# A hybrid decoder step on one core: memory scores inside the attention's tail, the first roots ahead of the page numbers, and the first piece of each sample step ahead of the recurrence's finish

## The chip, the cores and the metric

The program runs on one core of one Trainium2 chip. Its time is device microseconds for one execution of the whole step, from the first to the last instruction with the little that lies around it. The engines are TensorE (PE, with its weight loads as PEld), VectorE (DVE), ScalarE (ACT), GpSimd (POOL) and the queue engine SyncE (SP). A measurement is the median of three runs.

## What is computed

Two layers, each on 2048 prompt rows and on 8 sample rows (one new token for each of eight sequences). A layer normalises its input, projects it to 3360 columns, and feeds four head groups: a short gated convolution, an RWKV-7 recurrence, latent attention (causal for the prompt, over 4096 cached tokens for the samples), and cross-attention into 256 memory tokens. Cut to what matters here:

```
for l in range(DEPTH):
    mk, mv = mem_kv(mem_prompt, mem_norm_g[l], w_mem_k[l], w_mem_v[l])      # rms_norm, two projections
    xp, ... = trunk_layer(xp, pos_p, ..., mk, mv, prompt_attend, p)
    ckv_past = cache_ckv[l, page_table].reshape(Bs, -1, KV_RANK)
    xs, ... = trunk_layer(xs, pos_s, ..., cache_mem_k[l], cache_mem_v[l], make_sample_attend(...), p)

def mem_attend(q, mem_k, mem_v):
    s = jnp.einsum('bshd,bmhd->bhsm', qh, mem_k).astype(jnp.float32) * (HEAD_DIM ** -0.5)
    pr = jax.nn.softmax(s, axis=-1).astype(q.dtype)
    return jnp.einsum('bhsm,bmhd->bshd', pr, mem_v).reshape(B, S, MEM_W)

mixed = concat([conv_out * silu(c_gate), rwkv_out * silu(r_gate), mla_out * silu(mla_gate), mem_out * silu(mem_gate)])
x = x + rms_norm(einsum('bse,ed->bsd', mixed, w_out), post_g)
```

## The kernel before

Each engine has its own program, written out by hand; engines meet only through semaphores (`s_...`). The order of an engine's work is the order of its code. A layer is a prologue and eight blocks of 256 prompt rows (`block(B, m, e)`, with `m = 0..3`, `e = 0, 1`, block number `2m + e`), then a short pass for the samples. "Block 4 of layer 0" below is `m = 2, e = 0`.

**A block on PE** is `project`, `rwkv_chunks`, `attention`, `attention_out`, `memory`, `project_out`. PE is a line of small fp32 matmuls. In the traces all of them stand at line 815 (`mm`) or, for transposes, at line 819 (`tr`), so they are told apart by their tiles: `bank<-kv,Q` are attention scores, `bank<-cst,Sm` the transposes of probabilities (`turn(c)`), `bank<-memKT,mq` the memory's scores, `bank<-kv,cst` and `bank<-kv,wuq` the products of a sample step. Some instructions have two records each.

**The attention** of a block works through `n = 8(m+1)` chunks of scores. `scores(c)` fills one of five banks in rotation (`score_bank`: 0, 1, 7, 6, 5); DVE takes the row maximum (`masked_max`), ACT the exponentials (`probs`, L2645, into `Sm`), PE turns them (`turn(c)`, which waits for `probs(c)`), ACT copies them out (`take(c)`, L2655 to L2667) and PE multiplies with the values (`values(x)`). PE runs five chunks of scores ahead. In the last five chunks there are no scores left to issue between two turns: this is the tail. ACT alternates `probs(c+1)` and `take(c)`. In the blocks with `m = 0`, `take(4)` also waits for `values(0)`.

**Behind the tail**, `attention_out` (L1217) issues `memory_scores(B, 0)` and `(B, 1)` into banks 0, 1 and 6, 7, the recurrence's mean (`group_norm`), two gate tiles (25 and 26) and, between them, four transposes of `T3` into bank 5, which wait for `s_on`: DVE has to have the inverse row sums ready. DVE's `memory_max(B, j)` comes after its attention work and the inverse sums (L2277). `memory` turns the memory's probabilities and multiplies with `memV`. `project_out` multiplies eight row groups `k` with `w_out`, in the order of `i0 = 0..7`; the weights for `i0 = 4` are loaded once `i0 = 0` is done.

**Sample steps.** The samples' work is spread over the blocks: PE does it between two groups of `project_out` (`sample_step`), DVE after `rwkv_finish`. Block 0: squares (L2000, L2001), PE sums them at `i0 = 1`, POOL takes the roots (L2862), DVE scales, PE projects the queries at `i0 = 3`. Block 1: keys (L2041 to L2054), summed at `i0 = 2`. Blocks 2 and 3: `spread` (L2103), used at `i0 = 2`. `rwkv_finish` (L1894 to L1901) starts when ACT has the inverse root of the variance (L2552), and its result is needed at `i0 = 6`.

**Prologue of layer 0.** DVE scales the mean squares of the memory rows (L1569), POOL raises them to the power -1/2 (`memory_roots`, L2776), DVE scales the rows (L1571), PE turns them (`turn_memory`), DVE copies them out with their gain (L1580), and PE makes the memory's keys and values with `w_mem_k` and `w_mem_v`. On POOL, four loads of the page numbers and their conversion (L2765, L2767) stand ahead of those roots; the conversion waits for the loads. The numbers are first used by POOL's own `gather` in block 0's recurrence.

Of the kernel before, what the change touches and what calls it, by code (L numbers as in the profile page):

```python
# [19 lines left out]
P = 128  # L20
# [141 lines left out]
def build_program(nc, a):  # L162
    ctx = ExitStack()
    with ctx:
# [383 lines left out]
        def score_bank(c):  # L548

            return (0, 1, 7, 6, 5)[c % 5]  # L550

# [261 lines left out]
        def _(pe):  # L813
# [347 lines left out]
            def attention(B, l, m, e):  # L1161
# [55 lines left out]
            def attention_out(B):  # L1217

                if B.prompt:
                    memory_scores(B, 0)  # L1220
                    memory_scores(B, 1)
# [3 lines left out]
                    for i in range(4):  # L1225
                        last = tr(PP[5][:, i * P:(i + 1) * P], flat3(T3)[:, i * P:(i + 1) * P], P)
# [9 lines left out]
            def memory_scores(B, j):  # L1236
                J = slice(j * P, (j + 1) * P)
                for h in range(2):
                    q = slice(64 * h, 64 * h + 64)
                    for p in range(2):  # L1240
                        last = mm(PP[6 * j + h][:, p * NM:(p + 1) * NM], mq[q, p, J], memKT[q, p, :])
                last.then_inc(s_ms.h, 1)

            def memory(B):
                def turn(j):
                    pe.wait_ge(s_mn.h, s_mn.at(B.ip, j + 1))
                    b0 = 6 * j
                    for q in range(4):
                        for t in range(2):
                            last = tr(PP[b0 + q // 2][:, (q % 2) * T + t * P:(q % 2) * T + (t + 1) * P],  # L1250
# [294 lines left out]
        def _(v):  # L1545
# [357 lines left out]
            def attention(B, l, m, e):  # L1903
# [37 lines left out]
            def gate_attention(B):  # L1941
                n = B.n
                v.wait_ge(s_uv.h, s_uv.at(B.ot, 1))
                if B.prompt:
# [3 lines left out]
                    v.tensor_tensor(x, x, halves(5, n), MULT).then_inc(s_uvr.h, 1)  # L1948
# [4 lines left out]
            def memory_max(B, j):  # L1953
                top, neg, _, _ = mst[j]
                v.wait_ge(s_ms.h, s_ms.at(B.ip, j + 1))
                for h in range(2):
                    v.tensor_reduce(top[:, 2 * h:2 * h + 2], halves(6 * j + h, T), AX, MAX)
# [37 lines left out]

            def sample_latents(B, scaled):

                l, n = B.l, NS
                v.wait_ge(s_pa.h, s_pa.at(B.ip, NTILES))
                v.tensor_tensor(ssq[:, 0, :], sproj[:, 7, :], sproj[:, 7, :], MULT)  # L2000
                v.tensor_tensor(ssq[:, 1:3, :], sproj[:, 9:11, :], sproj[:, 9:11, :], MULT).then_inc(s_sdv.h, 1)  # L2001
# [35 lines left out]
            def sample_prepare(B, scaled):  # L2037

                l = B.l
# [9 lines left out]
                kx, rx = spr[:, 2:4, :], spr[:, 0:2, :]  # L2049
                drain()  # L2050
                v.tensor_tensor(sT1, kx, scalars(V("kk", 0, 2), NS), MULT)
                v.tensor_tensor(su, sproj[:, 15:17, :], sproj[:, 13:15, :], MULT)
                drain()
                v.tensor_tensor(sT2, sT1, sT1, MULT).then_inc(s_sdv.h, 1)  # L2054
# [52 lines left out]
            def sample_states(B, steps, turned):  # L2107

                l = B.l
                if steps[0] == 0:  # L2110
                    v.wait_ge(s_sac.h, s_sac.at(l, SAC["decay"]))
                    v.wait_ge(s_sl.h, s_sl.at(l, s_sl.n))
                for i in steps:
                    spread(l, i)
# [131 lines left out]
            for l in range(L):  # L2246
# [26 lines left out]
                def block(B, m, e):  # L2273
# [3 lines left out]
                    memory_max(B, 0)  # L2277
# [623 lines left out]
```

## Time and profile before

| | us |
|---|---|
| runs of before | 3522.21, 3518.31, 3515.10 (median 3518.31) |
| the profiled execution | 3512.8 |
| its span, first to last instruction | 3511.0 |
| PE busy in it | 3400.2 (97%) |
| DVE / ACT / POOL busy | 2023.6 / 1267.0 / 243.9 |

The profiled execution is 5.5 us faster than the median of the three runs. A row of the timeline gives start, duration, engine, line, operation, output and inputs; the bracket at its end is the time that the engine was idle before it, and what released it.

### The profile page before, as it was taken

The numbers are of one execution on the slowest core, as the hardware profiler recorded it, in microseconds if no ns is written. First come the engines' busy times: TensorE is split into PE (matmuls) and PEld (weight loads), VectorE is DVE, ScalarE is ACT, GpSimd is POOL, SyncE is SP. The second block draws the span as 40 slices with busy tenths as digits, with TensorE's granted clock in tenths as the row PEclk, the third lists the DMA queues.
The fourth block names the chain that finished last, engine by engine and source line by source line (L and its number), as shares of the span: only waits on it lengthen the run. The fifth ranks groups of instructions, "written<-read, shape, count | busy, mean of one in ns | idle before, by whom it ended". The sixth has DMA issues, their size and how long they took to land.

```text
span 3511.0 us, 80468 instructions
## 1 busy us (share of the span) xinstructions
PE 3400.2 (97%) x33076; PEld 2591.2 (74%) x33076; DVE 2023.6 (58%) x5212; ACT 1267.0 (36%) x3599; POOL 243.9 (7%) x284
## 2 busy tenths in 40 slices
PE   7999999999999999999999999999999999999998
PEld 5768686877869678686567786868778687776864
DVE  3656565665656556565356566656656565464653
ACT  2323334242343423524433233332423434234343
POOL 3200100000010000000040001000000000000000
PEclk9999999999999999999999999999999999999999
DMA  7654453625436153252365634536263351632512
GB/s 218 208 175 158 144 189 108 200 88 184 135 122 206 51 200 123 102 192 69 106 216 174 201 127 173 155 115 210 63 231 115 117 186 49 236 110 91 194 55 68
DMA packets 281024, 514.82 MB, mean 147 GB/s; under 512 B 30037, under 2 KB 215571, under 8 KB 268115
## 3 DMA queue, kind: packets, MB, share of 16 engines
q1 hardware_dynamic: 258903, 463.96, 40.3%
q0 software_dynamic: 11648, 41.95, 3.4%
q8 instruction: 263, 4.31, 0.5%
q10 hardware_dynamic: 10108, 3.76, 0.4%
q14 instruction: 102, 0.84, 0.1%
HBM read 473.15 MB, written 47.49 MB: 148 GB/s over the span
## 4 chain that ended last, share of the span: by engine, by line
PE 86%; ACT 5%; DVE 4%; issue 2%; DMA 2%; DVEq 1%; ACTq 1%; POOL 0%; SPq 0%; POOLq 0%
PE bank L815 78%; PE bank L819 7%; DVEq L1548 1%; DMA win<-in_w_in 1%; DMA wout<-in_w_out 1%; ACT Q L2575 1%; ACT PT L2690 0%; ACT Sm L2645 0%; ACT qr L2574 0%; DVE mix L1778 0%; ACTq L2551 0%; ACT L2552 0%; ACT Q L2573 0%; DVE swaa L1776 0%; DVE mix L1774 0%
## 5 line engine op out<-in xcount | busy, mean ns | idle before, releaser
L815 PE MATMUL bank<-hT,win 128*128 128x256 f32 (+3 forms) x6384 | 1188.1, 339 | 5.4 <-DMA win<-in_w_in 2.7
L815 PEld LDWEIGHTS bank<-hT,win 128*128 128x128 f32 (+1 forms) x6384 | 949.2, 186 | 143.1 <-issue 34.7
L815 PE MATMUL bank<-wout,win 128*128 128x128 f32 x3136 | 379.9, 276 | 0.0
L815 PEld LDWEIGHTS bank<-wout,win 128*128 128x128 f32 x3136 | 364.6, 192 | 1.0
L815 PE MATMUL bank<-kv,Q 96*128 96x512 f32 (+3 forms) x640 | 276.4, 529 | 0.2
L1915 DVE TENSOR_REDUCE ml<-bank 128x1 f32<-128x512 f32 (+3 forms) x320 | 195.3, 610 | 124.1 <-PE bank L815 113.7
L819 PEld LDWEIGHTS bank<-cst,Sm 128*128 128x128 f32 x1344 | 157.6, 141 | 145.9 <-issue 67.4
L819 PE MATMUL bank<-cst,Sm 128*128 128x128 f32 x1344 | 210.7, 278 | 24.9 <-ACT Sm L2645 18.0
L2645 ACT ACTIVATE Sm<-bank,ml 128x512 f32<-128x512 f32 (+3 forms) x320 | 200.1, 626 | 76.8 <-DVE ml L1920 70.8
L815 PE MATMUL bank<-wout,mix 128*128 128x512 f32 x480 | 218.4, 605 | 2.2 <-DMA wout<-in_w_out 1.3
L815 PEld LDWEIGHTS bank<-wout,mix 128*128 128x128 f32 x480 | 89.8, 192 | 109.6 <-issue 107.9
L2541 ACT ACTIVATE mix<-bank 128x512 f32<-128x512 f32 (+1 forms) x68 | 39.7, 597 | 351.3 <-PE bank L815 351.3
L2421 ACT ACTIVATE mix<-bank 128x256 f32<-128x256 f32 x128 | 49.2, 384 | 307.8 <-PE bank L815 307.8
L2820 POOL DMA_INDIRECT G<-in_cache_ckv,idc x32 | 31.7, 989 | 1574.6 <-PE bank L815 1569.7
L815 PEld LDWEIGHTS bank<-kv,Q 96*128 96x128 f32 x640 | 101.4, 192 | 22.8 <-issue 15.0
L2428 ACT ACTIVATE mix<-bank 128x128 f32<-128x128 f32 x98 | 27.0, 276 | 227.8 <-PE bank L815 209.9
L815 PE MATMUL bank<-PT,XX 64*64 64x64 f32 x2560 | 100.7, 231 | 7.4 <-ACT PT L2584 4.3
L815 PE MATMUL bank<-PT,mix 128*128 128x512 f32 x224 | 102.7, 602 | 0.0
L815 PE MATMUL bank<-XX,mix 128*128 128x512 f32 x224 | 101.3, 595 | 0.0
L815 PE MATMUL bank<-XX,PT 64*64 64x64 f32 x2048 | 93.1, 218 | 0.0
L815 PEld LDWEIGHTS bank<-PT,XX 64*64 64x64 f32 x2560 | 71.0, 133 | 27.4 <-ACT PT L2584 21.4
L1802 DVE TENSOR_TENSOR OO<-OO,cst 128x256 f32<-128x256 f32 x160 | 63.6, 422 | 47.0 <-PE bank L815 43.4
(527 smaller groups left out, 5952.3 us busy)
## 6 DMA issues: line engine op xcount, KB each, us to landing
win<-wfast SPq DMA_DIRECT2D x98, 1024.0 KB, 6.7
win<-in_w_in SPq DMA_DIRECT2D x78, 1024.0 KB, 5.6
win<-wfast SPq DMA_DIRECT2D x98, 768.0 KB, 6.1
wout<-in_w_out SPq DMA_DIRECT2D x60, 512.0 KB, 7.8
out_xres<-xin SPq DMA_DIRECT2D x16, 1024.0 KB
win<-in_w_in SPq DMA_DIRECT2D x16, 896.0 KB, 4.9
PT<-in_w_out SPq DMA_DIRECT2D x28, 512.0 KB, 3.8
XX<-in_w_out SPq DMA_DIRECT2D x28, 512.0 KB, 4.6
```

The source lines that it names most:

```text
L815: return pe.matmul(out, lhsT, rhs, start=start, stop=stop, skip_group_check=True)
L819: return pe.transpose(out, in_, ident[0:w, 0:w])
L1548: v.drain()
L1802: v.tensor_tensor(Om[j], An[j], mlev[:, lev + 1:lev + 2, :].broadcast_to([P, NH, 64]), MULT).then_inc(s_om.h, 1)
L1915: v.tensor_reduce(top, bank[:, 0:w], AX, MAX)
L2421: act.activation(o, PP[bank][0:o.shape[0], 0:T], ACT.Copy).then_inc(s_pa.h, tiles)
L2428: act.activation(first[i % 2], PP[tile_bank(PAIRS[i])][:, 0:P], ACT.Copy).then_inc(s_p1.h, 1)
L2541: last = act.activation(junk[0:w, (2 * j + i) * 512:(2 * j + i + 1) * 512], PP[B.bank + 2 * j + i][r0 * i:r0 * i + w, :], ACT.Square, accu ...
L2575: act.activation(Q96[NOPE:NOPE + RD, H, :], x[NOPE + RD:P], ACT.Copy).then_inc(s_qpr.h, 1)
L2645: act.activation(Sm[:, c % 2, 0:w], PP[score_bank(c)][:, 0:w], ACT.Exp, bias=rneg[:, row:row + 1], scale=MLA_SCALE, accum_out=psum[:, row, ...
L2820: pool.indirect_dma_start(dst, None, a[cache].rearrange("l n (g k) r -> (l n g) (k r)", g=g), bass.IndirectOffsetOnAxis(ap=idc[:, q, b:b + ...
```

## The change

Three edits, all in the order of work; nothing is computed otherwise.

1. `memory_scores(B, 0)` follows `turn(n - 4)` and `memory_scores(B, 1)` follows `turn(n - 2)`, in the banks that the chunks `n - 5` to `n - 2` have left; the transposes of `T3` go to the bank of chunk `n - 1`. DVE's two `memory_max` move ahead of the inverse sums.
2. POOL takes the roots of memory and of the first rows before it converts the page numbers.
3. `sample_head` does the first piece of a sample step (squares; keys; `spread(0)` or `spread(3)`) ahead of `memory_out` and `rwkv_finish`.

```diff
+        def freed_banks(m):
+            return [score_bank(8 * (m + 1) + i) for i in range(5)]
+        def memory_bank(m, j, h):
+            return freed_banks(m)[2 * j + h]
...
                     if c + 5 < n:
                         scores(c + 5)
+                    if c in (n - 4, n - 2):
+                        memory_scores(B, (c - n + 4) // 2)
                     if c > m and (c - m) % 4 == 0:
...
                 if B.prompt:
-                    memory_scores(B, 0)
-                    memory_scores(B, 1)
                     group_norm(B, 0)
                     tile(B, 25)
                     pe.wait_ge(s_on.h, s_on.at(B.ip, 1))
                     for i in range(4):
-                        last = tr(PP[5][:, i * P:(i + 1) * P], flat3(T3)[:, i * P:(i + 1) * P], P)
+                        last = tr(PP[freed_banks(B.m)[4]][:, i * P:(i + 1) * P], flat3(T3)[:, i * P:(i + 1) * P], P)
...
                         scale_rows(B, scaled)
                         scaled += 1
+                memory_max(B, 0)
+                memory_max(B, 1)
                 v.wait_ge(s_ae.h, n0 + n)
                 v.tensor_reduce(rsum, psum[:, :, 0:m + 1], AX, ADD)
...
+            def sample_head(B):
+                l = B.l
+                if B.block == 0:
+                    latent_squares(B)
+                elif B.block == 1:
+                    sample_keys(l)
+                elif B.block in (2, 3):
+                    if B.block == 2:
+                        v.wait_ge(s_sac.h, s_sac.at(l, SAC["decay"]))
+                    spread(l, 0 if B.block == 2 else 3)
...
                     if B.block > 3 and B.turns:
                         turn_rows(B, 0, 8)
+                    sample_head(B)
                     memory_out(B)
                     rwkv_finish(B)
...
-            pool.wait_ge(s_pg.h, 16 * 4)
-            pool.tensor_copy(pgf[:, :], pgi[:, :])
-            pool.drain()
-            pool.tensor_scalar(pgf[:, :], pgf[:, :], 4.0, K("sub"), MULT, ADD)
-            pool.drain()
...
                 x_roots(l * IT, 1)
                 x_roots(l * IT + 1)
 
+                if l == 0:
+                    pool.wait_ge(s_pg.h, 16 * 4)
+                    pool.tensor_copy(pgf[:, :], pgi[:, :])
+                    pool.drain()
+                    pool.tensor_scalar(pgf[:, :], pgf[:, :], 4.0, K("sub"), MULT, ADD)
+                    pool.drain()
```

`latent_squares` is the wait for the projections and the two squares of `sample_latents`; `sample_keys` is the head of `sample_prepare` up to the squares of the keys, without the convolution's product. Both go out of their old places.

On PE, the tail of block 4 of layer 0 (24 chunks). `Sm` are turned probabilities of chunks 19 to 23, four, four, two, four and four transposes; `memKT,mq` are the memory's scores. Before:

```order
2239 L819 MATMUL bank3<-cst,Sm 128x128 x4
2240 L819 MATMUL bank2<-cst,Sm 128x128 x4
2241 L819 MATMUL bank3<-cst,Sm 128x128 x2
2242 L819 MATMUL bank2<-cst,Sm 128x128 x4
...
2255 L819 MATMUL bank3<-cst,Sm 128x128 x4
...
2272 L815 MATMUL bank0<-memKT,mq 128x256 x2
2273 L815 MATMUL bank1<-memKT,mq 128x256 x2
2274 L815 MATMUL bank6<-memKT,mq 128x256 x2
2275 L815 MATMUL bank7<-memKT,mq 128x256 x2
2276 L815 MATMUL bank2<-cxs,cst 128x512
```

The same place in the changed kernel:

```order
2239 L827 MATMUL bank3<-cst,Sm 128x128 x4
2240 L827 MATMUL bank2<-cst,Sm 128x128 x4
2241 L823 MATMUL bank5<-memKT,mq 128x256 x2
2242 L823 MATMUL bank0<-memKT,mq 128x256 x2
2243 L827 MATMUL bank3<-cst,Sm 128x128 x2
2244 L827 MATMUL bank2<-cst,Sm 128x128 x4
2245 L823 MATMUL bank1<-memKT,mq 128x256 x2
2246 L823 MATMUL bank7<-memKT,mq 128x256 x2
...
2276 L823 MATMUL bank2<-cxs,cst 128x512
```

Half of the memory's scores now stands between the turns of chunks 20 and 21, half behind that of chunk 22; the mean's product (`cxs,cst`) follows the last values at once.

On DVE, the end of block 1 of layer 0, from the gate of the memory group (`mix<-Bp,mix`) to the keys of the samples (`raw`, `kv`). Before:

```order
503 L1784 SCALAR_TENSOR_TENSOR mix<-Bp,mix 128x512 [waits gate_tanh_ready]
504 L1970 SCALAR_TENSOR_TENSOR mix<-mix,bank 128x512 [waits mem_values_done]
505 L1894 TENSOR_TENSOR cxs<-cxs,T 128x512 [waits square_root_done]
...
508 L1901 SCALAR_TENSOR_TENSOR mix<-mix,cxs 128x512
509 L2041 COPY raw<-sproj 128x16 x3
510 L2042 COPY raw<-sproj 128x8
511 L2044 TENSOR_TENSOR kv<-shs,raw 128x56
```

After:

```order
503 L1791 SCALAR_TENSOR_TENSOR mix<-Bp,mix 128x512 [waits gate_tanh_ready]
504 L2064 COPY raw<-sproj 128x16 x3
505 L2065 COPY raw<-sproj 128x8
506 L2067 TENSOR_TENSOR kv<-shs,raw 128x56
...
510 L2076 TENSOR_TENSOR kv<-kv 128x16
511 L1979 SCALAR_TENSOR_TENSOR mix<-mix,bank 128x512 [waits mem_values_done]
512 L1901 TENSOR_TENSOR cxs<-cxs,T 128x512 [waits square_root_done]
```

The keys and their squares stand ahead of the instruction that waits for `square_root_done`, where they stood behind it.

## Rows read from the trace of the kernel before

**Rows 1.** The page: busy time of each engine.

```profile
PE 3400.2 (97%) x33076; PEld 2591.2 (74%) x33076; DVE 2023.6 (58%) x5212; ACT 1267.0 (36%) x3599; POOL 243.9 (7%) x284
```

**Rows 2.** Waits of PE, whole span: us in total, times, longest.

```profile
PE bank L819 <- ACT Sm L2645: 18.0, 32, 1.1
...
PE bank L815 <- DVE kv L2001: 6.5, 2, 3.2
PE bank L815 <- DVE kv L2103: 3.9, 4, 1.0
...
PE bank L815 <- ACT XX L2655: 1.1, 4, 0.3
```

**Rows 3.** Timelines of DVE, POOL and PE in the prologue.

```profile
11.21 0.15 DVE L1569 TENSOR_SCALAR st<-st 128x1 f32<-128x1 f32 x1
...
15.34 0.19 POOL L2765 CAST pgf<-pgi 128x8 f32<-128x8 int32 x1 [6.41 <-DMA pgi<-in_page_table]
...
16.57 0.58 POOL L2776 TENSOR_TENSOR st<-st,mhalf 128x1 f32<-128x1 f32 x1 [0.15 <-issue]
...
17.98 3.68 PE L819 MATMUL bank<-cst,hT 128*128 128x128 f32 x16 [7.54 <-DVE hT L1571]
22.54 12.55 PE L815 MATMUL bank<-kv 128*128 128x512 f32 x24 [0.88 <-DVE kv L1580]
```

**Rows 4.** Issue and landing (us from issue) of the memory's value weights.

```profile
3.38 1.63 SPq L583 DMA_DIRECT2D kv<-in_w_mem_v  x1
...
kv<-in_w_mem_v SPq DMA_DIRECT2D x1, 1024.0 KB, 13.4
```

**Rows 5.** Timelines of PE and DVE: tail of block 4, then a turn outside tails.

```profile
1004.66 0.44 PE L819 MATMUL bank<-cst,Sm 128*128 128x128 f32 x2 [0.71 <-ACT Sm L2645]
1005.82 0.66 PE L819 MATMUL bank<-cst,Sm 128*128 128x128 f32 x4 [0.72 <-ACT Sm L2645]
...
1007.62 0.43 DVE L1938 COPY T<-ml 128x512 f32<-128x512 f32 x1 [0.42 <-PE bank L815]
...
1010.35 2.10 PE L815 MATMUL bank<-memKT,mq 64*128 64x256 f32 x16
...
1016.80 0.60 PE L819 MATMUL bank<-cst,T 128*128 128x128 f32 x4
...
1414.30 0.33 PE L819 MATMUL bank<-cst,Sm 128*128 128x128 f32 x1 [0.64 <-ACT Sm L2645]
```

**Rows 6.** Timeline of ACT, block 1: `take(4)`.

```profile
378.66 0.38 ACT L2664 ACTIVATE T<-bank 128x256 f32<-128x256 f32 x1 [0.21 <-PE bank L815]
```

**Rows 7.** Timeline of PE in `project_out` of blocks 0 and 1, layer 1 last.

```profile
206.68 0.81 PE L815 MATMUL bank<-kv,cst 128*128 128x8 f32 x6 [3.24 <-DVE kv L2001]
207.34 5.38 PE L815 MATMUL bank<-wout,mix 128*128 128x512 f32 x8
212.55 3.60 PE L815 MATMUL bank<-PT,mix 128*128 128x512 f32 x8
215.99 1.85 PE L815 MATMUL bank<-kv,wuq 128*128 128x8 f32 x16
...
407.59 0.37 PE L815 MATMUL bank<-kv,cst 128*128 128x16 f32 x2 [1.43 <-DVE kv L2054]
...
2148.31 0.37 PE L815 MATMUL bank<-kv,cst 128*128 128x16 f32 x2 [1.73 <-DVE kv L2054]
```

**Rows 8.** Stretches: busy time of PE, PEld, DVE, ACT, POOL; then granted clock.

```profile
208.00:210.00 2.00, 2.00 (x4) 0.75 (x3) 0.00 (x0) 0.00 (x0) 2.00 (x1) 0.50 0.99 411
...
410.00:412.00 2.00, 2.00 (x6) 0.95 (x5) 1.92 (x6) 0.00 (x0) 2.00 (x1) 1.00 1.06 420
...
2150.00:2152.00 2.00, 2.00 (x4) 0.85 (x3) 2.00 (x7) 0.00 (x0) 1.90 (x1) 0.50 1.01 404
```

**Rows 9.** Timelines of DVE and POOL, block 0: recurrence's finish, roots.

```profile
203.33 0.69 DVE L1894 TENSOR_TENSOR cxs<-cxs,T 128x512 f32<-128x512 f32 x1 [2.46 <-ACT T L2552]
...
207.85 2.93 POOL L2862 TENSOR_TENSOR kv<-kv,mhalf 128x16 f32<-128x16 f32 x1 [5.42 <-DVE kv L2010]
```

More of the change, by code:

```diff
@@ L1240, in memory_scores @@
                     for p in range(2):
-                        last = mm(PP[6 * j + h][:, p * NM:(p + 1) * NM], mq[q, p, J], memKT[q, p, :])
+                        last = mm(PP[memory_bank(B.m, j, h)][:, p * NM:(p + 1) * NM], mq[q, p, J], memKT[q, p, :])
                 last.then_inc(s_ms.h, 1)
@@ L1246, in turn @@
                     pe.wait_ge(s_mn.h, s_mn.at(B.ip, j + 1))
-                    b0 = 6 * j
                     for q in range(4):
                         for t in range(2):
-                            last = tr(PP[b0 + q // 2][:, (q % 2) * T + t * P:(q % 2) * T + (t + 1) * P],
+                            last = tr(PP[memory_bank(B.m, j, q // 2)][:, (q % 2) * T + t * P:(q % 2) * T + (t + 1) * P],
                                       Pm[j][:, q, t * P:(t + 1) * P], P)
@@ L1947, in gate_attention @@
                     drain()
-                    v.tensor_tensor(x, x, halves(5, n), MULT).then_inc(s_uvr.h, 1)
+                    v.tensor_tensor(x, x, halves(freed_banks(B.m)[4], n), MULT).then_inc(s_uvr.h, 1)
                     return
@@ L1956, in memory_max @@
                 for h in range(2):
[L1957 removed]
+                    v.tensor_reduce(top[:, 2 * h:2 * h + 2], halves(memory_bank(B.m, j, h), T), AX, MAX)
                 drain()
@@ L1994, in residual, with latent_squares @@
                     drain()
-            def sample_latents(B, scaled):
-                l, n = B.l, NS
+            def sample_head(B):
[8 more added lines that the diff above has]
+                    spread(l, 0 if B.block == 2 else 3)
+            def latent_squares(B):
                 v.wait_ge(s_pa.h, s_pa.at(B.ip, NTILES))
@@ L2001, in sample_latents @@
                 v.tensor_tensor(ssq[:, 1:3, :], sproj[:, 9:11, :], sproj[:, 9:11, :], MULT).then_inc(s_sdv.h, 1)
+            def sample_latents(B, scaled):
+                l, n = B.l, NS
                 v.tensor_copy(smq[:, :, :], sproj[:, 11:13, :])
@@ L2035, in sample_latents, with sample_keys @@
                 drain()
-            def sample_prepare(B, scaled):
-                l = B.l
+            def sample_keys(l):
                 for i, t in ((0, 3), (2, 1), (4, 5)):
@@ L2048, in sample_prepare @@
                 v.tensor_tensor(spr, raw[:, :, :], sT3, ADD).then_inc(s_sdv.h, 1)
-                kx, rx = spr[:, 2:4, :], spr[:, 0:2, :]
+                kx = spr[:, 2:4, :]
                 drain()
                 v.tensor_tensor(sT1, kx, scalars(V("kk", 0, 2), NS), MULT)
+                drain()
+                v.tensor_tensor(sT2, sT1, sT1, MULT).then_inc(s_sdv.h, 1)
+            def sample_prepare(B, scaled):
+                l = B.l
+                kx, rx = spr[:, 2:4, :], spr[:, 0:2, :]
                 v.tensor_tensor(su, sproj[:, 15:17, :], sproj[:, 13:15, :], MULT)
                 drain()
-                v.tensor_tensor(sT2, sT1, sT1, MULT).then_inc(s_sdv.h, 1)
                 for p in range(2):
@@ L2110, in sample_states @@
                 if steps[0] == 0:
-                    v.wait_ge(s_sac.h, s_sac.at(l, SAC["decay"]))
                     v.wait_ge(s_sl.h, s_sl.at(l, s_sl.n))
                 for i in steps:
-                    spread(l, i)
+                    if i != steps[0]:
+                        spread(l, i)
                     if i in turned:
@@ L2276, in block @@
                     scaled = attention(B, l, m, e)
-                    memory_max(B, 0)
-                    memory_max(B, 1)
                     centre(B)
@@ L2682, in block @@
                         for q in range(4):
-                            last = act.activation(Pm[j][:, q, :], PP[6 * j + q // 2][:, (q % 2) * T:(q % 2) * T + T], ACT.Exp,
+                            last = act.activation(Pm[j][:, q, :], PP[memory_bank(m, j, q // 2)][:, (q % 2) * T:(q % 2) * T + T], ACT.Exp,
                                                   bias=mst[j][1][:, q:q + 1], scale=MEM_SCALE, accum_out=mst[j][2][:, q:q + 1])
@@ L2689, in block @@
                         for q in range(2):
-                            last = act.activation(PTm[j][:, q, :, :], PP[6 * j + q][:, :].rearrange("p (a t) -> p a t", a=4), ACT.Copy)
+                            last = act.activation(PTm[j][:, q, :, :], PP[memory_bank(m, j, q)][:, :].rearrange("p (a t) -> p a t", a=4), ACT.Copy)
                         last.then_inc(s_mtr.h, 1)
```

## The prediction

> **What bounds the kernel now.** I read the busy times first: PE works 3400.2 of 3511.0 us, every other engine under 60% [rows 1]. So only two things can shorten the run: PE's idle time, 111 us in all, and PE's own slow stretches. Next I read the list of PE's waits, of which the edits aim at the largest [rows 2], then the timelines around each, to see what the waiting engine's releaser was itself waiting for, and last the granted clock in the stretches where the same product takes two different times [rows 7, 8]. The diff keeps every product, so PE's 3400.2 us stay but for the clock.
>
> **Edit 2, the roots in the prologue.** DVE's mean squares are there at 11.21 + 0.15 = 11.36, but POOL begins the root at 16.57 [rows 3]. In between stands the conversion of the page numbers, which waited 6.41 us for its transfer and began at 15.34. With the root ahead it can begin at about 11.45: 5.1 us earlier. Everything behind is a chain (DVE's scaling, PE's turns after 7.54 us idle, DVE's copies, the keys' and values' products at 22.54), and the compute rows down that chain give no other wait, so the 5.1 go through. Two things could cut it. The products would begin at 22.54 − 5.1 = 17.4, and the value weights land at 3.38 + 13.4 = 16.8 [rows 4]: 0.6 to spare. The conversion now follows the last root and delays POOL's later sums of the first block by about a microsecond; what they feed leaves through the queue, and PE asks for it in the recurrence, microseconds later: nothing. The page numbers are used in block 0's recurrence. If transfers bind instead I bound the gain below by 2, a landing 3.7 later with products not before 20.5, and above by 5.2, the whole distance from 11.36 to 16.57. I take **−5.1**.
>
> **Edit 1, memory's scores in the tail.** PE waits 18.0 us for probabilities, 32 times [rows 2]. Going through the turns block by block, 28 of them lie in tails; the four others are 0.64 [rows 5] and 0.42, in both layers, 2.1 us, which leaves 15.8 in tails. In the tail ACT needs about as long for `probs(c+1)` and `take(c)` as PE for a turn and its values, or longer, and PE has nothing to put between. The memory's scores last 2.10 us, 1.05 for each half [rows 5]. They are work that PE has to do anyway, so a wait of up to 1.05 in front of which a half stands vanishes. In blocks 0 to 3, 6 and 7 a half covers what it stands ahead of. In block 4 the waits are 0.71 and 0.72 [rows 5], in block 5 together as much, and in each of them both lie between the turns n−4 and n−2, where only the first half stands: 1.43 − 1.05 = 0.38 is left, four times, −1.5. In blocks 0 and 1 `take(4)` already waits 0.21 for the values [rows 6], and those now come behind a half: I charge 0.3 in the two tails where it is latest, in each layer one, −0.6. The four waits for `take`'s last copies, 1.1 [rows 2], end in the same stretch and are covered by the second half. Sum 15.8 − 1.5 − 0.6 + 1.1 = **−14.8**. Upper bound 15.8 + 1.1 = 17. Lower bound 7: each half could shift the wait to the next turn, because what binds is ACT's chain and not PE's order; then only the waits at the second half's place and behind it go, about half.
>
> The edit moves DVE's two `memory_max` ahead of the inverse sums, on which the transposes of `T3` wait. In block 4 DVE starts the copy for them at 1007.62 and PE turns them at 1016.80 [rows 5]. The second maximum now needs the second half, over at about 1008, and some 1.5 us of DVE; sums, inverse and copy take another 1.5: ready at some 1011. PE does the same work ahead of these transposes in another order, without the waits of 1.43 us, and comes there at 1016.80 − 1.43 = 1015.4. Some 4 us are left: cost nothing. The banks are those of chunks whose probabilities have been taken before the turn ahead.
>
> **Edit 3, the first pieces of the sample steps.** The waits that it aims at are 6.5 (squares, twice 3.24), 3.2 (keys, 1.43 and 1.73) and 3.9 (`spread`, four of about 0.98) [rows 2, 7]: 13.6. In each DVE did the piece behind `rwkv_finish`, which lasts from 203.33 to about 206.3 in block 0, and which itself waited 2.46 us for ACT [rows 9]. In that idle time fit the squares (about 0.3), `spread` (about 1.4) and nearly the keys (about 1.9): so neither `memory_out`'s product, which PE needs only at `i0 = 4`, nor `rwkv_finish`, needed at `i0 = 6`, comes later. All 13.6 go.
>
> The clock is the second gain. After the wait of 3.24 the eight products that follow take 5.38 and the next eight 3.60 [rows 7], and the granted clock of that stretch is 0.50, the 1.2 GHz level, where it is 1.00 (2.4 GHz) after the wait of 1.43 [rows 8]. It is 0.50 again after the wait of 1.73 in block 1 of layer 1 [rows 8]. With block 0 of layer 1 that is three falls, each worth 5.38 − 3.60 = 1.78: 5.3 us, which go when the waits do.
> The Trainium skill ("TensorE: Matmul & The Clock Gate", section "Why this matters for your kernels") advises to leave no idle gap of PE above about 3 µs, since one such drops the clock. By it the two gaps of 3.24 explain a fall and that of 1.73 does not, so a third fall would stay: the sum would be 1.8 less, about 3482. The trace shows the fall behind 1.73 as well, and I go by the trace.
>
> Against it a new wait. The queries at `i0 = 3` need the roots, 9.31 us behind the squares' sums (215.99 − 206.68) [rows 7], 7.5 with the clock up. The sums now come at 203.44, so PE is at the queries at about 210.95. DVE takes the sums up only behind `rwkv_finish`, as before at 207.6, POOL's root takes 2.93 from 207.85 [rows 9], and DVE's scaling ends at about 211.2. New wait 0.3, twice: −0.6. The weights of `i0 = 4`, ordered when `i0 = 0` is done, have until then 14.3 us, as now in blocks without a wait, where they cost 0.7 at most; that goes in the range. Sum 13.6 + 5.3 − 0.6 = **−18.3**, bounds 13.0 (no clock back) and 18.9.
>
> **Sum.** 5.1 + 14.8 + 18.3 = 38.2. The profiled execution took 3512.8, so 3474.6; the median of the runs stands 5.5 above it, so **3480** for the median. With all lower bounds, 22, it is 3496, with all upper ones, 5.2 + 17 + 18.9 = 41.1, it is 3477. The three runs of before lie 7 us apart; I allow 3 for a median.
>
> **Rivals.**
> The tail gives half. Each half of the scores delays the values behind it, so ACT's `take` and with it the next `probs` come later, and the wait stands again one turn further on. For it: `take(4)` is already waiting [rows 6], and in block 4 two waits follow each other [rows 5]. Against: ACT has in the tail only `probs` and `take`, and `take(c)` needs the turn alone, not the values, except in the blocks with `m = 0`. 7.4 lost: 3487, chance 0.12.
> The prologue is bound by transfers. The value weights leave 0.6 [rows 4], and a landing later by 2 to 3 us than before gives 3483; chance 0.07.
> The clock is not gained, because other short waits of the same stretch (the new one at the queries) make it fall: 5.3 lost, 3485; chance 0.08.
> Slower: the inverse sums come too late. They stand behind both maxima, and the second maximum behind PE's second half. Once they slip by more than the 4 us of margin, PE waits for them in all 16 blocks; the gain of 38.2 is gone at 38.2 / 16 = 2.4 us a block, a slip of 4 + 2.4 = 6.4 in place of the 3 that I work out. At a slip of 7.6 it is 3.6 a block, 57.6 − 38.2 = 19 slower: 3537. For it: the copy for these transposes starts at 1007.62 only after 0.42 us of waiting for PE [rows 5], so DVE has no lead there. Against: from 1011 to 1015.4 two more maxima would fit. Chance 0.03.
> The order doesn't bind as I read it, and everything that goes from the waits comes back elsewhere in the same block (PT's or the gates' copies on ACT, transfers of weights): within 0.2%; chance 0.02.
>
> **How the numbers follow.** My forecast has 0.68, the three rivals that are faster than before too 0.12 + 0.07 + 0.08 = 0.27, the two last 0.05. 0.2% is 7 us, about what a measurement of this kernel can tell from no change; the forecast lies 38 below, and even all lower bounds leave 22. So faster has 0.95, within 0.02, slower 0.03. The likeliest case gives 3480 with 3474 to 3486 by its unknown costs and the spread of the medians; the range reaches to the rivals at 3483 to 3487 and to a pair of them together at 3492: 3471 to 3493; outside it I leave the two last cases and, of the others, sizes beyond their bounds.
>
> **What would show it.** In the changed profile PE's list should have no wait for the squares or keys and at most a few tenths for `spread`; its wait for probabilities should fall from 18.0 to about 4, of which 2.1 outside the tails and 1.5 in blocks 4 and 5. PE's first transposes should stand at about 12.9 instead of 17.98. In the stretches of `project_out` of blocks 0 and 1 the clock should read 1.00 and eight products 3.60. A new row of about 0.3, for the scaled squares, should stand in block 0. `T3`'s transposes should have no wait. I am wrong if the probabilities' wait stays above 9, if a wait for the inverse sums appears in many blocks, or if PE's busy time doesn't fall by about 5 us.

## The result and the profile after

| | before | after |
|---|---|---|
| median of four runs each, us | 3516.70 | 3479.70 |
| lowest and highest, us | 3513.84, 3522.21 | 3477.17, 3481.01 |
| the profiled execution, us | 3512.8 | 3480.4 |
| its span, us | 3511.0 | 3478.6 |

The ratio is 0.9896, with an interval from 0.988 to 0.9913: the change makes the kernel 37.0 us faster by the medians, and 32.4 us by the two profiled spans. The forecast was 3480, from 3471 to 3493.

The page of the kernel after, busy time of each engine, answers to [rows 1]:

```profile
PE 3399.5 (98%) x33076; PEld 2589.1 (74%) x33076; DVE 2030.8 (58%) x5212; ACT 1264.2 (36%) x3599; POOL 243.5 (7%) x284
```

PE does the same 33076 instructions and is busy 0.7 us less. So nearly all of the 32.4 us comes out of its idle time. The waits of PE in the kernel after (us in total, times, longest) answer to [rows 2]; line numbers are those of the new code, L2673 is the old L2645:

```profile
PE bank L827 <- ACT Sm L2673: 4.5, 12, 0.6
...
PE bank L823 <- DVE st L2349: 4.2, 2, 2.1
...
PE bank L823 <- DVE st L2265: 3.4, 2, 1.9
...
PE bank L823 <- ACT hT L2426: 3.2, 2, 1.6
PE bank L827 <- DVE hT L1578: 2.7, 1, 2.7
...
PE bank L823 <- ACT XX L2683: 0.8, 4, 0.2
...
PE bank L823 <- DVE kv L2038: 0.3, 1, 0.3
```

The wait for probabilities is 4.5 instead of 18.0 us, 12 times instead of 32. The squares (6.5), the keys (3.2) and `spread` (3.9) are gone from the list; in their place stands one wait of 0.3 for the scaled squares (`kv L2038`). The prologue's wait for the scaled rows is 2.7 instead of 7.54 [rows 3]. The wait for `take`'s last copies (`XX`) is 0.8 instead of 1.1. Together that is 13.5 + 13.3 + 4.8 + 0.3 = 31.9 us.

Timelines of PE in the prologue, the tail of block 4 (with the DVE copy that the transposes of `T3` wait for) and `project_out` of block 0:

```profile
13.15 3.68 PE L827 MATMUL bank<-cst,hT 128*128 128x128 f32 x16 [2.74 <-DVE hT L1578]
17.70 12.56 PE L823 MATMUL bank<-kv 128*128 128x512 f32 x24 [0.88 <-DVE kv L1587]
...
990.92 1.14 PE L823 MATMUL bank<-memKT,mq 64*128 64x256 f32 x8
992.00 0.44 PE L827 MATMUL bank<-cst,Sm 128*128 128x128 f32 x2
992.86 0.66 PE L827 MATMUL bank<-cst,Sm 128*128 128x128 f32 x4 [0.42 <-ACT Sm L2673]
993.44 1.14 PE L823 MATMUL bank<-memKT,mq 64*128 64x256 f32 x8
...
996.60 0.43 DVE L1947 COPY T<-ml 128x512 f32<-128x512 f32 x1
1002.88 0.60 PE L827 MATMUL bank<-cst,T 128*128 128x128 f32 x4
...
199.30 3.68 PE L823 MATMUL bank<-wout,mix 128*128 128x512 f32 x8
202.81 3.60 PE L823 MATMUL bank<-PT,mix 128*128 128x512 f32 x8
206.66 1.92 PE L823 MATMUL bank<-kv,wuq 128*128 128x8 f32 x16 [0.25 <-DVE kv L2038]
208.76 5.40 PE L823 MATMUL bank<-XX,mix 128*128 128x512 f32 x8
```

The prologue's transposes stand at 13.15 instead of 17.98, 4.8 earlier. In block 4 the first of the two waits [rows 5] is gone and 0.42 of the second is left. The copy for `T3` ends at 997.03, 5.8 us ahead of its transposes. In block 0 the products behind the squares' sums now take 3.68, but those behind the queries take 5.40 instead: the slow stretch has moved, not gone.

Granted clock (the third number from the right) in stretches of the kernel after; the columns are those of [rows 8]:

```profile
209.50:213.00 3.50, 3.50 (x5) 1.33 (x4) 3.40 (x10) 0.00 (x0) 0.00 (x0) 0.51 0.38 156
...
1739.00:1745.00 6.00, 4.50 (x13) 0.83 (x14) 2.98 (x11) 0.00 (x0) 1.08 (x2) 0.50 0.33 110
1770.00:1776.00 6.00, 5.57 (x13) 4.34 (x14) 0.39 (x3) 0.38 (x2) 1.26 (x1) 0.50 0.69 228
1926.00:1946.00 20.00, 20.00 (x68) 10.01 (x66) 12.72 (x36) 3.24 (x7) 4.64 (x3) 1.00 0.82 304
2124.00:2144.00 20.00, 19.91 (x57) 9.16 (x56) 14.31 (x47) 0.95 (x5) 3.10 (x1) 1.00 0.88 327
```

`project_out` of blocks 0 and 1 of layer 1 (the last two) is at 1.00, the 2.4 GHz level, throughout. Two long stretches between the layers, where the edits change nothing, are at 0.50; the profile of before has a single one of 3.4 us there.

### The profile page after: what moved, and what is told of

Read it like the earlier page. It is cut to its first block, busy times and chain, and to the rows that moved or that the text cites. A ratio compares the mean times of both kernels' runs of the same rounds, so it can differ in the third digit from the quotient of the medians.

```text
span 3478.6 us, 80470 instructions
## 1 busy us (share of the span) xinstructions
PE 3399.5 (98%) x33076; PEld 2589.1 (74%) x33076; DVE 2030.8 (58%) x5212; ACT 1264.2 (36%) x3599; POOL 243.5 (7%) x284
## 4 chain that ended last, share of the span: by engine, by line
PE 88%; ACT 4%; DVE 3%; issue 2%; DMA 2%; DVEq 1%; POOL 0%; ACTq 0%; POOLq 0%; SPq 0%
PE bank L823 81%; PE bank L827 7%; DMA win<-in_w_in 1%; DVEq L1555 1%; DMA wout<-in_w_out 1%; ACT Q L2603 1%; ACT PT L2718 1%; ACT qr L2602 0%; DVE mix L1785 0%; ACT Sm L2673 0%; ACT Q L2601 0%; DVE swaa L1783 0%; DVE mix L1781 0%; ACT hT L2426 0%; ACT PT L2523 0%
## 5 line engine op out<-in xcount | busy, mean ns | idle before, releaser
L2673 ACT ACTIVATE Sm<-bank,ml 128x512 f32<-128x512 f32 (+3 forms) x320 | 199.8, 625 | 76.8 <-DVE ml L1927 70.0
L827 PE MATMUL bank<-cst,Sm 128*128 128x128 f32 x1344 | 210.7, 278 | 11.4 <-ACT PT L2523 5.9
```

The source lines that it names most:

```text
L827: return pe.transpose(out, in_, ident[0:w, 0:w])
L2673: act.activation(Sm[:, c % 2, 0:w], PP[score_bank(c)][:, 0:w], ACT.Exp, bias=rneg[:, row:row + 1], scale=MLA_SCALE, accum_out=psum[:, row, ...
```

## Experiments

**Each edit alone, and all of them again.** The three edits are those of the diff ahead, each put alone into the kernel before; edit 1 is everything on `memory_scores`, `memory_max` and the banks, edit 2 the move of the page numbers, edit 3 `sample_head`. Timed on one chip.

> The kernel before with edit 1 alone (memory's scores in the attention's tail, maxima ahead of the inverse sums). My theory: the wait for probabilities falls from 18.0 to 4.5 us and the one for take's copies from 1.1 to 0.8, as in the changed kernel, nothing else moves: 13.8 less, 0.39% (ratio 0.9961). Rival, part of this gain depends on the other edits: 10 or less. Granted clock: the fall in block 0 stays where it was (squares' wait), so no clock gain.

> The kernel before with edit 2 alone (roots ahead of the conversion of the page numbers). My theory: 4.8 less (ratio 0.9986), PE's first transposes at about 13.1. Rival, the transfers take it back behind the first projections: under 2 less.

> The kernel before with edit 3 alone (first pieces of the sample steps). Waits gone 13.6, new 0.3: 13.3 less if the clock gives nothing (ratio 0.9962). By the prediction's clock term, 18.3 less (ratio 0.9948). In the profile the two theories differ at blocks 0 and 1 of layer 1 and block 0 of layer 0: by the prediction the clock is 1.00 throughout there; by the rival, that falls come where they come in each execution, there is a fall there or elsewhere and the sum of the stretches at 0.50 stays near 14 us outside the last 20.

> The changed kernel again, timed beside the three single edits. The sum of their gains is the gain of all: 13.8 + 4.8 + 13.3 = 31.9, to which the medians add up to 37.0 at most; ratio 0.9895 to 0.9909. If the falls of the clock belong to waits, its profile shows them at the places of the first one (block 0 of layer 0, and between the layers, twice as long as before); if not, at other places or in another number.

| | median, us | to before (3516.44) | ratio, interval | span in the profile, to 3511.0 |
|---|---|---|---|---|
| edit 1 | 3501.08 | -15.4 | 0.9965, 0.9951 to 0.9978 | 3495.0, -16.0 |
| edit 2 | 3512.70 | -3.7 | 0.9987, 0.9978 to 0.9996 | 3513.0, +2.0 |
| edit 3 | 3498.76 | -17.7 | 0.9956, 0.9942 to 0.9969 | 3497.3, -13.7 |
| all | 3481.00 | -35.4 | 0.9903, 0.9888 to 0.9918 | 3479.2, -31.8 |

The three gains by the medians add up to 36.8, all together to 35.4: within what the intervals can tell, the edits don't help or hinder each other. Edit 3's 17.7 lies between the two values that its expectation sets against each other, 13.3 without a gain of the clock and 18.3 with one, and its interval holds both. Edit 1 alone has the same 4.5 us of waits for probabilities, edit 3 alone the same single 0.25 in block 0. Edit 2 shows why a single profile misleads. Its span is longer than that of before, though the wait that it aims at went as forecast:

```profile
13.00 3.67 PE L819 MATMUL bank<-cst,hT 128*128 128x128 f32 x16 [2.67 <-DVE hT L1571]
```

What it lost in that execution stands in its granted clock, between the layers, where before has one stretch at 0.50 of 3.4 us:

```profile
1756.00:1762.00 6.00, 5.26 (x14) 0.97 (x16) 2.35 (x9) 0.00 (x0) 1.09 (x2) 0.50 0.13 34
1787.00:1793.00 6.00, 5.95 (x14) 4.61 (x15) 0.57 (x4) 0.00 (x1) 1.00 (x1) 0.50 0.66 222
```

So I summed the time at 0.50 in every profile by place, up to the end of the span:

| us at 0.50 | first 100 us | blocks 0 and 1, layer 0 | between the layers | blocks 0 and 1, layer 1 | last 30 us | elsewhere |
|---|---|---|---|---|---|---|
| before | 0 | 3.4 | 3.4 | 6.8 | 6.2 | 0 |
| edit 1 alone | 0 | 3.4 | 6.8 | 3.4 | 12.1 | 0 |
| edit 2 alone | 0 | 6.8 | 13.7 | 6.8 | 6.3 | 0 |
| edit 3 alone | 0 | 3.4 | 13.7 | 0 | 6.4 | 0 |
| after | 0 | 3.4 | 13.7 | 0 | 5.9 | 0 |
| after again | 0 | 0 | 13.7 | 0 | 9.4 | 0 |
| squares back (below) | 3.4 | 3.4 | 6.8 | 0 | 9.4 | 0 |
| scores in pieces | 0 | 0 | 10.2 | 0 | 9.0 | 0 |
| maxima four times | 0 | 10.2 | 10.2 | 6.8 | 9.1 | 20.5 |
| maxima twice | 10.2 | 0 | 6.8 | 3.4 | 6.1 | 0 |
| maxima behind | 0 | 3.4 | 13.7 | 0 | 9.5 | 0 |
| filled (f4) | 0 | 3.4 | 3.4 | 0 | 2.9 | 0 |
| filled short (f5) | 3.4 | 6.8 | 3.4 | 0 | 2.5 | 0 |
| filled at three places (f6) | 6.8 | 0 | 0 | 0 | 3.4 | 0 |

The same kernel has 3.4 us in block 0 in one execution and none in the other. A stretch of 3.4 us at 0.50 costs half of that, 1.7 us, the 5.38 for 3.60 of [rows 7].

A profile shows one execution. The mean granted clock over the span is on record for nearly every run, to three decimals, and one minus that clock, times the span, is the time lost to the clock if PE is busy throughout. A step of 0.001 is 3.5 us, too coarse for one run; the mean over some runs says more (the error is that of the mean):

| | runs | mean time, us | lost to the clock | time without it |
|---|---|---|---|---|
| before (three chips) | 31 | 3515.6 | 16.0 ± 0.5 | 3499.6 |
| edit 1 | 5 | 3500.9 | 16.1 ± 1.4 | 3484.8 |
| edit 2 | 11 | 3511.7 | 15.6 ± 1.0 | 3496.1 |
| edit 3 | 5 | 3498.9 | 10.5 ± 1.1 | 3488.4 |
| all three edits, both times | 8 | 3480.0 | 11.3 ± 1.1 | 3468.7 |
| squares back | 5 | 3490.4 | 16.0 ± 1.8 | 3474.4 |
| scores in pieces | 4 | 3495.0 | 12.2 ± 3.0 | 3482.8 |
| maxima four times | 4 | 3538.5 | 30.1 ± 1.0 | 3508.4 |
| maxima twice | 4 | 3478.8 | 10.4 ± 1.4 | 3468.4 |
| maxima behind | 4 | 3481.6 | 13.0 ± 0.9 | 3468.5 |
| filled (f4) | 4 | 3480.5 | 6.1 ± 0.9 | 3474.5 |
| filled short (f5) | 4 | 3477.8 | 7.0 ± 1.4 | 3470.8 |
| filled at three places (f6) | 4 | 3475.4 | 5.2 ± 1.0 | 3470.2 |

The 47 runs of kernels without edit 3 lose 15.9 us to the clock on average, the 25 of kernels with it and with no added wait or filling 11.4: edit 3 brings 4.5 us, give or take 0.8, beside its waits. On the one chip where it ran alone beside 15 runs of before it is 10.5 against 16.4. Edits 1 and 2 alone bring nothing of the kind. Without the clock's share all three edits bring 30.9 us, against 31.9 of waits in the profiles.

**The squares back.** Only the first piece of block 0 goes back; keys and `spread` stay early.

```diff
             def sample_head(B):
-                if B.block == 0:
-                    latent_squares(B)
-                elif B.block == 1:
+                if B.block == 1:
                     sample_keys(l)
...
             def sample_latents(B, scaled):
+                latent_squares(B)
```

> The changed kernel with the squares of block 0 back behind the recurrence's finish, keys and spread still early. Waits: 6.5 more, 0.3 less, so 6.2 slower than the changed kernel. If the clock's fall in block 0 of layer 1 belongs to that wait, the granted clock is 0.50 there again (none in the two profiles of the changed kernel) and the price is 1.7 more, 7.9: against the kernel before 27 less by the medians. If falls come by themselves, no fall there.

The median is 3490.74 (ratio 0.9929, 0.9915 to 0.9942), 10 to 11 above the changed kernel's two medians, more than the 6.2 and the 7.9 of the expectation; the profiled span is 3484.0, 5.4 above. The list of waits has the two 3.24 again. In the profile the clock doesn't follow in layer 1. The window of block 0, layer 1, with the squares back (PE idle 1.1 us of its 3.24 in it):

```profile
1932.00:1940.00 8.00, 6.89 (x21) 3.58 (x22) 4.43 (x19) 0.00 (x0) 2.93 (x1) 1.00 1.01 403
```

and the timeline of PE in edit 1 alone, which also keeps both waits, in blocks 0 and 1 of layer 1:

```profile
1937.86 0.81 PE L823 MATMUL bank<-kv,cst 128*128 128x8 f32 x6 [3.24 <-DVE kv L2010]
1938.52 3.68 PE L823 MATMUL bank<-wout,mix 128*128 128x512 f32 x8
...
2136.85 0.37 PE L823 MATMUL bank<-kv,cst 128*128 128x16 f32 x2 [1.73 <-DVE kv L2063]
2137.06 5.38 PE L823 MATMUL bank<-PT,mix 128*128 128x512 f32 x8
```

Twice PE idled 3.24 us in block 0 of layer 1 and the clock stayed at 2.4 GHz; the shorter idle time of 1.73 was followed by a fall. Of the four executions with the 3.24 at that place two had a fall, and all four had one behind the same wait in block 0 of layer 0; of the three with the 1.73 all had one, of the three with the 1.43 in block 1 of layer 0 none. So a fall isn't tied to one wait, but how often it comes is: over all five runs the kernel with the squares back loses 16.0 us to the clock, as before, where the changed one loses 11.3. Of the 10 to 11 us of the medians, 5.7 are then waits (6.2 expected) and 4.7 the clock, which the profiled execution doesn't show; with five runs the second number is good to 2. With both pieces early and no added wait, eight of nine profiles have no fall at either place; the ninth, with maxima taken twice, has one in block 0 of layer 1 (1936 to 1939), where PE no longer waits for the squares.

**Memory's scores in smaller pieces.** An attempt to cover the 0.42 that is left in blocks 4 and 5.

```diff
-                    if c in (n - 4, n - 2):
-                        memory_scores(B, (c - n + 4) // 2)
+                    for piece in {n - 4: (0, 1), n - 3: (2,), n - 2: (3,)}.get(c, ()):
+                        memory_scores(B, *divmod(piece, 2))
...
-            def memory_scores(B, j):
+            def memory_scores(B, j, h):
-                for h in range(2):
-                    q = slice(64 * h, 64 * h + 64)
-                    for p in range(2):
+                q = slice(64 * h, 64 * h + 64)
+                for p in range(2):
```

> The changed kernel with the second half of memory's scores cut in two pieces, one after the turn n-3, one after the turn n-2. By the prediction's account of blocks 4 and 5 (both waits between the turns n-4 and n-2, 1.05 us of work there), another 0.53 us stands ahead of the second wait, so the four waits of 0.42 go: the wait for probabilities falls from 4.5 to about 2.8 us. Rival, ACT's chain sets the end of the tail and the wait moves on: it stays at 4.5 or stands at the next turn. In the time 1.7 us, less than can be told.

The wait fell to 2.5 us: the four 0.42 of blocks 4 and 5 went, as expected, and two of 0.20 with them. And yet the kernel came to 3494.00, 13 to 14 slower than the changed one (ratio 0.9943, 0.9925 to 0.9961): PE was busy 3413.1 us, 13.6 more. Timeline of PE in the tail of block 4:

```profile
991.30 1.14 PE L823 MATMUL bank<-memKT,mq 64*128 64x256 f32 x8
992.37 0.44 PE L827 MATMUL bank<-cst,Sm 128*128 128x128 f32 x2
992.74 1.13 PE L823 MATMUL bank<-memKT,mq 64*128 64x256 f32 x4
993.80 0.66 PE L827 MATMUL bank<-cst,Sm 128*128 128x128 f32 x4
994.38 1.13 PE L823 MATMUL bank<-memKT,mq 64*128 64x256 f32 x4
```

The group of all memory's scores (busy us, mean ns of one, idle time before) in this kernel:

```profile
L823 PE MATMUL bank<-memKT,mq 64*128 64x256 f32 x256 | 54.3, 402 | 0.0
```

and in the changed one:

```profile
L823 PE MATMUL bank<-memKT,mq 64*128 64x256 f32 x256 | 36.5, 402 | 0.0
```

Eight records take 1.14 us when the products on rows 0 to 63 and those on rows 64 to 127 (`h = 0` and `h = 1`) stand together, and four of one kind take 1.13. Each record lasts 402 ns either way; the two kinds together take the time of one. A half of 1.05 us can't be cut at `h`: the second half grows to 2.2, in 16 tails 17.8 us in all.

**The margin of the inverse sums (the slower rival).** Three kernels change how much DVE does ahead of them. The first takes each maximum four times, the second twice (`range(2)`).

```diff
                 top, neg, _, _ = mst[j]
                 v.wait_ge(s_ms.h, s_ms.at(B.ip, j + 1))
-                for h in range(2):
-                    v.tensor_reduce(top[:, 2 * h:2 * h + 2], halves(memory_bank(B.m, j, h), T), AX, MAX)
+                for rep in range(4):
+                    if rep:
+                        drain()
+                    for h in range(2):
+                        v.tensor_reduce(top[:, 2 * h:2 * h + 2], halves(memory_bank(B.m, j, h), T), AX, MAX)
```

> The changed kernel with each of the two maxima of a block taken four times ahead of the inverse sums (3 x 2 x 1.37 us more for DVE). Rival 4 measured: in block 4 of layer 0 the inverse sums are ready 5.8 us ahead of the transposes of T3 that wait for them. With 8.2 more they come 2.4 to 3 late, in up to 16 blocks: 38 to 48 slower than the changed kernel, about the kernel before. If the margin were larger than I read, no change.

> The changed kernel with each maximum taken twice (2 x 1.37 us more for DVE ahead of the inverse sums). By the margin of 5.8 us read in block 4, 2.7 us more cost nothing: within 3 us of the changed kernel, no wait for the inverse sums, against 58 us with each taken four times. Rival, blocks with fewer chunks have less margin: waits of some tenths there, and each may bring a fall of the clock: 3 to 12 slower.

In the third the two calls of `memory_max` stand where they stood before, behind the inverse sums:

> The changed kernel with DVE's two maxima back behind the inverse sums, memory's scores still in the tail. The inverse sums are ready 5.8 us ahead of their transposes in the changed kernel, so their place costs nothing; the maxima come 1 to 2 us later for ACT, whose exponentials PE needs only after tile 26. My theory: no change within 3 us, no new wait of PE. Rival: the maxima are what lets memory's part run on time, 16 waits of up to 1 us, 5 to 15 slower.

| | median, us | ratio, interval |
|---|---|---|
| maxima four times | 3538.46 | 1.0064, 1.0048 to 1.0079 |
| maxima twice | 3478.90 | 0.9898, 0.9881 to 0.9915 |
| maxima behind the sums | 3481.76 | 0.9906, 0.9890 to 0.9923 |

Twice costs nothing and shows no wait for the sums. Whether DVE takes the maxima ahead of the sums or behind them doesn't matter: that part of the edit is free and brings nothing. Four times is the rival in full, 58 us slower than the changed kernel, more than the 38 to 48 of the expectation, and 22 slower than before. The waits of PE in it:

```profile
PE bank L827 <- DVE T L1947: 24.2, 16, 3.1
PE bank L823 <- DVE T L1888: 10.9, 16, 0.7
```

They explain 35 us of 57 by the spans. The other part is PE's busy time, 3420.7, 21 more for the same instructions. In this kernel alone, stretches at 0.50 stand in the middle of the layers (20.5 us, table), each in a block where PE now waits over a microsecond, though not in every such block. In all it has 56.8 us at 0.50 in place of 23.0, which is 17 of the 21; the other 4 stay open. Over its four runs it loses 30.1 us to the clock in place of 11.3, 19 more.

**Filling PE's idle time between the layers.** The remaining question is what makes the clock fall at 1738 and 1769. PE waits 2.08 us for DVE, then 1.50 (the `st` rows of the list after), amid products with 8 columns of output. Three kernels put products there whose values nobody needs.

```diff
             def attention_out(B):
...
+                for i in range(4):
+                    mm(PP[4][:, :], ones, memV[:, :, :].rearrange("p a b -> p (a b)"))
                 pe.wait_ge(s_otr.h, s_otr.at(B.l, 1))
...
+                for i in range(3):
+                    mm(PP[4][:, :], ones, memV[:, :, :].rearrange("p a b -> p (a b)"))
                 pe.wait_ge(s_mix.h, s_mix.at(B.ot, 1))
                 for i0 in range(2, 6):
```

> The changed kernel with products whose result nobody reads put into two idle times of PE in the samples' pass at each layer's end: four of 128x512 ahead of the wait of 2.08 us, three ahead of that of 1.50. Theory A, an idle TensorE is what makes the clock fall there: the stretch at 0.50 of 6.8 us at the end of layer 0 (1738 to 1745) shrinks or goes, and so does the last but one of layer 1, while the one after the first projection's wait (1769 to 1776), which is not filled, stays; time 3 to 6 less than the changed kernel. Theory B, the falls come from the small products themselves (8 columns): nothing changes, or 0.5 slower.

Against what the expectation says, bank 4 holds the sums of the samples' projection at that place, and the filling overwrites them: the samples' values are other ones, while every other instruction is as in the changed kernel. Windows of this kernel:

```profile
1739.00:1745.00 6.00, 6.00 (x28) 2.11 (x28) 3.27 (x13) 0.00 (x0) 1.08 (x2) 1.00 0.17 49
1770.00:1776.00 6.00, 6.00 (x24) 4.97 (x24) 1.31 (x7) 0.45 (x2) 1.90 (x2) 0.85 0.56 186
```

Its timeline of PE, with the fillings (`memV,cst`) and the samples' projection behind them:

```profile
1735.13 3.70 PE L823 MATMUL bank<-memV,cst 128*128 128x512 f32 x8
...
1739.44 2.84 PE L823 MATMUL bank<-memV,cst 128*128 128x512 f32 x6
1742.21 3.61 PE L823 MATMUL bank<-win,smix 128*8 128x512 f32 x16
```

The filled stretch is at 1.00, and the samples' products take 3.61, where they took 6.07 in the changed kernel. The time is the same, though, 3480.53: the fillings last 3.70 + 2.84 us where the waits were 2.08 + 1.50. Over its runs 5 us less are lost to the clock, and the time without it is 6 longer. I had taken 0.45 us for a product that takes 0.92, since it leaves two records. So the next two are shorter, and go to partitions 64 to 127 of that bank, which the samples don't use: `mm(PP[4][64:128, :], ones[:, 0:64], ...)`, two ahead of the first wait, one and a half ahead of the second. The last kernel adds one and a half, `mm(PP[7][:, :], ones, cst[:, 0:512])` and one of 256 columns, ahead of the wait of 1.56 for the first rows of layer 1.

> The changed kernel with shorter fillings than in f4, into partitions of a bank that nobody reads (nothing of the result changes): two products of 128x512 (0.92 each, as f4's profile shows) ahead of the wait of 2.08, one of 512 and one of 256 columns ahead of that of 1.50, in each layer's samples' pass. Theory A, an idle TensorE makes the clock fall there and f4's longer filling ate what it gave back (12.6 us of products for 7.6 us of waits and 6.7 us of clock): the stretches at 0.50 at 1738 to 1745 and the last but one of the run are gone and the waits too, 5 to 6.5 less than the changed kernel, ratio to the kernel before 0.988. Theory B, in f4 the falls were away by chance: they are back in this profile, time as the changed kernel.

> As f5, and a product of 512 and one of 256 columns ahead of PE's wait of 1.56 for the first rows of layer 1. Theory A: the stretch at 0.50 at 1769 to 1776 (3.4 to 6.8 us long, in all profiles with the changed order) goes too, 1.7 to 3.4 less than f5. Theory B, it belongs to the short transposes and the wait of 0.60 ahead of it: it stays, time as f5.

| | median, us | lowest, highest | ratio, interval | span |
|---|---|---|---|---|
| two places | 3477.87 | 3474.54, 3480.82 | 0.9896, 0.9879 to 0.9912 | 3476.3 |
| three places | 3475.29 | 3474.63, 3476.58 | 0.9890, 0.9873 to 0.9906 | 3473.5 |

The window over the whole change of layer with three places filled, and that of the changed kernel:

```profile
1735.00:1780.00 45.00, 41.02 (x184) 23.52 (x179) 19.19 (x54) 18.50 (x52) 11.85 (x24) 1.00 0.45 134
```

```profile
1735.00:1780.00 45.00, 38.28 (x152) 21.59 (x152) 17.36 (x50) 16.41 (x45) 10.88 (x23) 0.85 0.38 117
```

The first two places are clear. All eleven profiles without filling have a fall at these two waits at the end of layer 0 (from 1738 on in the changed kernel), the three with it none, and at the end of layer 1 all eleven have a stretch at 0.50 ahead of the last one, the three none, though the small products are still all there: what the clock answers to here is idle time and not the products of 8 columns. The third place is open. Against what the last expectation says, not all profiles with the changed order have a fall there: of the nine that leave it unfilled, "squares back" and "maxima twice" have none. One profile with it filled and no fall can be chance, all the more as PE idled there all the same, for a load ahead of the filling:

```profile
1767.72 0.35 PE L823 MATMUL bank<-cst,Q 8*128 8x8 f32 x2 [2.23 <-DMA qr<-in_state_conv]
```

The gain with three places over the changed kernel is 4 to 6 us by the medians, 3 to 5 if each is taken against the kernel before on its own chip; all four of its runs lie below all eight of the changed kernel's (3476.95 is the lowest), but the intervals of the two ratios overlap. With two places it is 2 to 3 by the medians, less than the 5 to 6.5 that I expected. By the means of all runs the two-place kernel loses 7.0 us to the clock and the three-place one 5.2, in place of 11.3, and their time without the clock is 2.1 and 1.5 longer. Between two and three places these errors leave no difference.

## Why the prediction was right

**Edit 2**, 5.1: 4.8 in the profile, 3.7 by the median of edit 2 alone. The inputs landed 0.3 later in this execution, which is the difference. The products found the value weights in place with their 0.88 us of wait as before; that rival did not come.

**Edit 1**, 14.8: 13.8 of waits. The four waits in blocks 4 and 5 are 0.42 each where the working had 0.38. In block 0 of each layer 0.37 is left for the 0.3 of a late `take(4)`, but only 0.20 of it stands behind `take(4)`; the other 0.17 is ahead of turn n−4, where no half stands, and was there before. The step that failed is small: the waits for `take`'s last copies were to be covered, 1.1, and 0.8 of them are there. In block 0 the 0.20 stayed, since ACT's copy comes behind the last turn and that turn behind the second half; the 0.34 of block 3 went, and block 2 has a new 0.19, whose cause wasn't looked for. The rival by which half the gain is lost did not come. Alone the edit measured 15.4.

**Edit 3**, 18.3: 13.3 of waits, as the working had them (13.6 gone, 0.3 new; the second 0.3 did not come). The term of 5.3 for the clock was right in size and wrong in its working. Over all runs on record it measures 4.5, give or take 0.8. But I took each fall of one profile as belonging to the wait ahead of it, so that it goes when the wait goes, and that is not so for a single fall. A wait of 3.24 was twice passed at full clock, and in layer 0 five of the nine profiles with both pieces early and no added wait still have a fall in blocks 0 and 1. What the edit changes is how often falls come there: in those blocks of both layers the three profiles without edit 3 have 10.2 us at 0.50 on average, the nine with it 2.7. That the profile of before had just the mean of 10.2 at these places is luck. And my last sign of being wrong did come: PE's busy time fell by 0.7 and not by about 5. It was a poor sign, since it sets one execution against another, and before's was one with few falls at other places, 19.9 us at 0.50 in all where edit 2's had 33.6.

The rule of the Trainium skill that stood against this term ("TensorE: Matmul & The Clock Gate", "Why this matters for your kernels": no idle gap above some 3 µs) doesn't fit the traces as a boundary: 3.24 was followed by a fall six times of eight, with none in edit 1 alone and with the squares back, and 1.73 three times of three.

**The median.** By the spans the gain was 32.4, by my sum 38.2. Of the difference of 5.8, 1.0 is in the waits aimed at (the tail 1.0 and the prologue 0.3 less, the samples 0.3 more), 4.6 is the clock in these two executions (PE's busy time fell by 0.7, not by 5.3) and 0.2 the rest. By the medians the gain was 37.0, because before's profiled execution was a short one: its 19.9 us at 0.50 cost 10 us, where the 31 runs of before lose 16.0 on average. This is, to within half a microsecond, the distance of 5.5 between profile and median that I added without giving a reason. The changed kernel's profiled execution has 23.0 us at 0.50, 11.5 lost, close to the 11.3 of its runs. With the waits of the profile and the clock of all runs the gain is 31.9 + 4.5 = 36.4, for the 38.2 of the sum.

**The slower rival** is real: once the inverse sums come late enough, all 16 blocks wait and the kernel is slower than before. That its 3537, worked out for a slip of 7.6 us, lies so near the 3538.46 of the kernel with four maxima is luck. The waits were 35 us, 2.2 a block and not 3.6, and the clock added most of the rest. The margin in block 4 was read as 4 us and is 5.8.

## What to carry to other kernels

Where one engine bounds a kernel at 97%, go through its waits one by one, ask what independent work of the same engine could stand there, and subtract what still limits it: that predicted the 31.9 us of waits here to within 1 us. Cut such filling work only where its pieces don't run side by side; two products on different row halves of TensorE cost one. Price the clock from the mean clock of many runs, as how often it falls, and not from the falls of one profile; expect removed waits to bring more than their length and added ones to cost more.

## What the runs showed of the hardware

- Products on rows 0 to 63 and 64 to 127 of TensorE that stand next to each other run together: eight records in 1.14 us, four of one half in 1.13.
- The granted clock goes to 0.50 for 3.4 or 6.8 us, and not in the same places in two executions of the same kernel. It went there mostly around idle times of 1.1 to 3.2 us. With two idle times at the layer's end filled, none of three profiles has a fall there, where all eleven without filling have one.
- Removing 13.3 us of waits in `project_out` took 4.5 us, give or take 0.8, off the time lost to the clock (72 runs).
- Waits of 35 us, spread over 16 blocks, cost 57: 17 of it by the lower clock in the profile, 19 as a mean of four runs.
